# Dilated attention on one NeuronCore: the next pair's scores are issued in front of the values, and one head's exponentials in front of the turned copies

## What is computed

```
for g, (window, dil) in enumerate(((128, 1), (512, 4), (2048, 16))):   # 3 groups, 16 heads of 64
    s = q @ k.T * 64 ** -0.5 + bias        # causal, within the window, every dil-th key
    e = exp(s - max(s)); den = sum(e)
    o[g], lse[g] = (e / den) @ v, max(s) + log(den)
w = softmax(stack(lse), over the groups)
out = sum(w[g] * o[g] for g) @ w_out
```

## Time and profile before

| | kernel before |
|---|---|
| median of three executions | 3044.39 us |
| the profiled execution, own time | 3040.92 us |
| its span in the profile | 3039.1 us |
| TensorE busy | 2878.0 us, 95% of the span |
| VectorE busy | 1955.8 us, 64% |
| ScalarE busy | 1571.8 us, 52% |
| loop of dilated attention | 686.49 to 771.55 us, 85.06 us |
| mean granted TensorE clock | 0.98 of full |

### The profile page before, as it was taken

The page is one execution under the profiler, slowest core; times in us unless marked ns, Lnnn a source line. Parts: engine busy times, 40 slices in busy tenths (PEclk is TensorE's granted clock), DMA queues, the critical chain, the costliest instruction groups (busy, mean ns, idle before and its releaser), DMA issues.

```text
span 3039.1 us, 54812 instructions
## 1 busy us (share of the span) xinstructions
PE 2878.0 (95%) x19827; PEld 2641.6 (87%) x19827; DVE 1955.8 (64%) x3147; ACT 1571.8 (52%) x2874; POOL 23.1 (1%) x38
## 2 busy tenths in 40 slices
PE   7989999997899889999999999998899999999998
PEld 7978999995899879999999888887899999978886
DVE  4556455446444766996787555568599778855555
ACT  3435444446544655445776444455544477744444
POOL 0000000001000000000000000000000000000000
PEclk9999999998999989999999999999999999999999
DMA  6415555554455324454443555543445544455554
GB/s 212 160 64 183 185 186 174 180 172 77 139 185 184 127 86 151 166 161 156 142 139 127 191 190 190 192 164 105 132 160 166 166 140 139 140 172 189 192 190 149
DMA packets 131003, 480.14 MB, mean 158 GB/s; under 512 B 14608, under 2 KB 14608, under 8 KB 130480
## 3 DMA queue, kind: packets, MB, share of 16 engines
q1 hardware_dynamic: 126432, 460.38, 46.0%
q0 software_dynamic: 4432, 17.87, 2.4%
HBM read 477.02 MB, written 1.18 MB: 157 GB/s over the span
## 4 chain that ended last, share of the span: by engine, by line
PE 80%; DVE 13%; ACT 4%; issue 1%; DMA 1%; POOL 0%; DVEq 0%; ACTq 0%; SPq 0%; POOLq 0%
PE ps L1452 24%; PE ps L1454 23%; PE ps L1453 23%; DVE wl L779 5%; PE ps L1920 4%; ACT wh L362 2%; PE ps L1554 1%; DVE mh L1322 1%; DVE picks L1324 1%; PE ps L1700 1%; DVE arena L1146 1%; DVE mh L1316 1%; PE ps L1732 1%; PE ps L1886 0%; DVE picks L1346 0%
## 5 line engine op out<-in xcount | busy, mean ns | idle before, releaser
L779 DVE TENSOR_TENSOR wl<-raw,wh 128x1024 fp32r<-128x1024 f32 x878 | 1075.6, 1225 | 913.9 <-ACT wh L362 907.9
L362 ACT ACTIVATE wh<-raw 128x1024 fp32r<-128x1024 f32 x878 | 929.9, 1059 | 1291.9 <-PE ps L1454 1283.9
L1452 PE MATMUL ps<-xh,wh 128*128 128x256 f32 x4448 | 1288.9, 290 | 37.8 <-DVE wl L779 25.2
L1453 PE MATMUL ps<-xl,wh 128*128 128x256 f32 x4448 | 1260.6, 283 | 0.0
L1454 PE MATMUL ps<-xh,wl 128*128 128x256 f32 x4448 | 1260.0, 283 | 0.0
L1452 PEld LDWEIGHTS ps<-xh,wh 128*128 128x128 f32 x4448 | 854.8, 192 | 58.4 <-issue 37.3
L1453 PEld LDWEIGHTS ps<-xl,wh 128*128 128x128 f32 x4448 | 855.7, 192 | 0.3
L1454 PEld LDWEIGHTS ps<-xh,wl 128*128 128x128 f32 x4448 | 854.6, 192 | 0.0
L1452 PE MATMUL ps<-wh,mh 128*128 128x512 f32 x1264 | 500.6, 396 | 16.2 <-DVE ml L791 14.9
L1454 PE MATMUL ps<-wh,ml 128*128 128x512 f32 x1264 | 497.1, 393 | 0.0
L1453 PE MATMUL ps<-wl,mh 128*128 128x512 f32 x1264 | 496.4, 393 | 0.0
(11 more groups left out here) (275 smaller groups left out, 1857.8 us busy)
## 6 DMA issues: line engine op xcount, KB each, us to landing
raw<-stream_dram SPq DMA_DIRECT2D x878, 512.0 KB, 3.4
arena<-bias_scratch POOLq DMA_DIRECT2D x16, 384.0 KB, 6.7
arena<-norm_rows POOLq DMA_DIRECT2D x4, 1024.0 KB, 7.3
arena<-keys_dram POOLq DMA_DIRECT2D x2, 1024.0 KB, 5.1
arena<-ret_c_dram POOLq DMA_DIRECT2D x1, 1344.0 KB, 6.1
xr<-x_dram POOLq DMA_DIRECT2D x1, 1024.0 KB, 9.4
out_dram<-arena POOLq DMA_DIRECT2D x2, 512.0 KB, 2.9
arena<-rg_w_dram POOLq DMA_DIRECT2D x2, 256.0 KB, 2.9
```

What stands on the lines that cost most here:

```text
L362: A(wh[b % 2][:, :, :], raw[:, b % 4, :].rearrange("p (a b) -> p a b", a=DB), ACT.Copy) \
L779: V.tensor_tensor(wl[b % 2][:, :, :], raw[:, b % 4, :].rearrange("p (a b) -> p a b", a=DB), wh[b % 2][:, :, :].bitcast(F32), ALU.subtract) ...
L1452: M(out_ap, lh, rh, start=first, stop=False, skip_group_check=skip)
L1453: M(out_ap, lh, rl, start=False, stop=False, skip_group_check=skip)
```

## The change

Two orders change. On TensorE, `att_scores(1)` moves to before the loop, and in the loop `att_scores(p + 2)` stands behind the two `att_turn` and in front of `att_values(p)`. As a sequence the only difference is that scores of pair p+1 and values of pair p-1 have changed places. On ScalarE, `exps(2p + 2)` moves from behind `turned(2p + 1)` to in front of `turned(2p)`. No instruction is added or removed, no wait inside a step is changed, and VectorE, GpSimd and SyncE keep their orders.

```diff
@@ ScalarE
             for p in range(DB):
+                if p + 1 < DB:
+                    exps(2 * p + 2)
                 turned(2 * p)
                 turned(2 * p + 1)
                 if p + 1 < DB:
-                    exps(2 * p + 2)
                     exps(2 * p + 3)
                 outs(p)
@@ TensorE
             att_scores(0)
+            att_scores(1)
             for p in range(DB):
-                if p + 1 < DB:
-                    att_scores(p + 1)
                 att_turn(2 * p)
                 att_turn(2 * p + 1)
+                if p + 2 < DB:
+                    att_scores(p + 2)
                 att_values(p)
```

## The result

The changed kernel takes 3051.22 us (median of 22 runs, 3046.32 to 3054.74), the kernel before 3044.20 us in the same sessions (22 runs, 3039.28 to 3050.28). The ratio is 1.0023, with an interval of 1.0016 to 1.0029, so it is 5 to 9 us slower. The prediction was 3051.0 us.

What follows compares the result with a forecast made beforehand. No engine was full; a back-and-forth chain bound each pair of the attention loop. Order gave -0.65 us, 4.5 more slow-clock spells 7.3, together +6.6 on 3044.39: 3051.0 us, range 3043.2 to 3054.5.

Steps and rivals of the forecast that it cites:

- full-clock pair: One pair of the dilated attention loop at full clock was to take 8.66 us, 0.1 below 8.77.
- second circle: Chain through TensorE in a pair: second turn, scores, values, outs, next exponential, first copy; 8.66 us, ending last by a hair.
- gap of 2.0 us: TensorE idle before each pair's second turn, in place of 0.78 and 1.34 us; the clock falls in nearly all pairs.
- price of a spell: A stretch of lowered TensorE clock was to lengthen a pair by 1.6 us, with bounds 0 and 3.1.
- Number of spells: Eight or nine stretches of lowered clock instead of four, 4.5 x 1.61 = 7.3 us; chance 0.57.
- rival's number (five to seven): Clock falls in only part of the loop's pairs: +1 to +4.2 us, 3045.4 to 3048.6; chance 0.2.
- Start and end: At full clock, the loop's start was to be 0.84 us shorter and its end 0.85 us longer.
- 6.1 us: 0.2% of the kernel's time, about what a measurement can tell from no change; slower by more had chance 0.48.
- Ten spells: Case of ten or longer stretches of lowered clock in the loop, chance 0.04; ten were put at 3054.1 us.
- stretch from scores to values: Rival: this TensorE stretch, not the gap, decides the clock; three to five spells, 3042.1 to 3045.4 us; chance 0.1.
- clock that stays up: Rival: TensorE's run of values, scores and turn holds full clock, four spells go, 3037.3 us; chance 0.06.
- Late maxima: Rival: scores p+2 wait on `a_b` for VectorE in front of values; 3046.7 to 3049.7 us; chance 0.03.

Runs made afterwards that it cites:

- kernel with all spells out: Changed kernel plus two products in front of each turn 2p and twelve between scores 0 and scores 1: 3040.74 us, ratio to before 0.9990.
- two counter-experiments: Two products in front of each turn 2p, added to the changed kernel (3041.24 us, ratio 0.9983) and to the kernel before (3043.88 us, ratio 1.0002).

## Why the prediction was right, step by step

- *The full-clock pair.* Reckoned 8.66, measured 8.54 wherever the gap was filled. The term that was too large is the way from the first copy to the second turn. I took 0.75 from the earlier trace rows, but behind an exponential a part of the copy lies beside the exponential's end. In the kernel with all spells out the copy begins at 716.46 and the exponential's last step ends at 716.55. The chain shows 0.49 + 0.14 = 0.63.
- *The second circle ends last.* Right, the chain shows it. `outs` stands in it and VectorE doesn't.
- *One gap of 2.0 us, and the clock falls behind it in nearly every pair.* Right: 1.97 us, and five pairs in a row at 0.83. The two counter-experiments (shorter gap in the same order; same work where it shortens no gap) carry this: the gap is what the change added and what had to be shortened. They don't show that its length alone decides. Nor does the sum of the idle time: it is 2.12 us in a pair before and 1.97 in one of the changed kernel, which has more spells. Behind 1.84 us (one pair) and behind 2.34 us (ScalarE's half, four pairs) the turn ran at full clock, and in the kernel before the same two gaps came with a fall in three pairs and without in the three that follow. That the gaps of before were "close to the edge" was argued from one execution.
- *The price of a spell.* 1.6 reckoned, 10.17 - 8.54 = 1.63 measured.
- *Number of spells.* Eight or nine reckoned, eight counted: in the second turns of pairs 0 to 6, and in the values of pair 6. At the places where I had counted them there are only seven, six in the middle and one at the end. The eighth is in turn 1, where I had none. The last values, which I counted at half clock, ran at full. Seven would have been the rival's number (five to seven), so the agreement is in part luck.
- *Start and end.* From the start of the loop to exps 3 it was to be 0.84 shorter. It was 1.27 longer (691.00 to 708.88, against 686.49 to 703.10), since scores 0 ran at half clock in this execution (3.73 instead of 2.28) and turn 1 had a spell, which I hadn't placed there. Scores 0 stand ahead of anything that the change moves, and were slow in profiles of either order, so their 1.45 us are chance. Exps 3 to exps 15 took 60.54 instead of 57.27, +3.3, where 4.2 was reckoned (three more spells, less 0.66), and the end 12.34 instead of 11.18, +1.2, where 3.3 was (one and a half more spells, and 0.85). Together +5.7 in the profile of the loop against +6.6 reckoned. The three terms were off by 2.1, 0.9 and 2.1 us, and part of their agreement is luck. The medians moved by 7.0, and the interval of the ratio has 1.002 in it, so on which side of the 6.1 us the change lies isn't settled.
- *A slip in the sums.* Ten spells give 3044.39 + 6 x 1.61 - 0.65 = 3053.4 us, and not 3054.1. The 0.65 had been left out.
- *The rivals.* The stretch from scores to values as what counts: out, by the eight spells, by the transposes and by the two lengths of gap. A clock that stays up: out as it stood, but so in the same order with the gap at 1.48 us. Late maxima: not in the full change, but a real wait of 1.54 us in TensorE's half alone, where exps and turned copies come sooner. I had seen nothing for it.
- *What I didn't forecast*: that the two halves have opposite signs, -7 to -9 us and +20 us, and that the first alone beats both kernels. The prediction treated the change as one.
- *The rule of the Trainium skill* ("TensorE: Matmul & The Clock Gate", Part 4: PE-mode transpose), that a transpose does not count as busy in the same way, doesn't hold here. Ten transposes and five products of the same length had the same effect (loops of 81.48 and 81.51 us at clock 1.00 in the pairs).

## What to carry to other kernels

When an order is changed on an engine that feeds TensorE, draw TensorE's idle time of a period before and after. The sum may stay the same while two gaps become one, and here one gap of 1.97 us cost a spell of half clock in each period, while 0.78 and 1.34 did so in four of eight. Try each half of a change alone, since here one gave 8 us and the other took 20. Work that TensorE does for nothing, put where it only shortens a gap, is worth a try: 0.43 us of it took the clock's fall away.

## What the hardware showed that I had not expected

- How little was enough: in one order of work, pairs with a gap of 1.97 us had a spell one after another, and five in a row with 1.48 us had none. The pairs with a spell can't be taken as trials of their own, since each stands behind another with one, and a gap of 1.84 us (one pair) left the clock up, so no edge in the gap's length can be read from this.
- Once the clock falls, the spell makes the pair 10.17 us long, and the next pair falls at nearly the same place. The spells came back in each of these pairs. In the kernel before, three pairs of 10.28 to 10.37 us were followed by three of 8.77 with the same work and the same gaps. Why the spells lock in one case and stop in the other isn't shown by a run.
- In the gap of this loop ten transposes kept the clock up like five products of the same duration.
